# A rotary embedding whose swapped copy is made by ScalarE copies of 32 rows, in place of a TensorE product with a turning matrix

## What is computed

```
def rope(x, pos):
    d = x.shape[-1]
    inv = ROPE_THETA ** (-jnp.arange(0, d, 2, dtype=jnp.float32) / d)
    ang = pos.astype(jnp.float32)[..., None] * inv
    cos = jnp.cos(ang)[:, :, None, :]
    sin = jnp.sin(ang)[:, :, None, :]
    xf = x.astype(jnp.float32)
    x1, x2 = xf[..., : d // 2], xf[..., d // 2:]
    return jnp.concatenate([x1 * cos - x2 * sin, x2 * cos + x1 * sin], axis=-1).astype(x.dtype)
```

## Time and profile before

| what | value |
|---|---|
| runs of the kernel | 2344.1, 2350.22, 2351.34 us (median 2350.22) |
| span of the profiled execution, first to last instruction | 2342.2 us |
| TensorE matmuls | 2255.8 us busy, 96% of the span |
| VectorE | 921.2 us, 39% |
| ScalarE | 381.2 us, 16% |
| mean granted TensorE clock | 0.982 of full speed |

### The profile page before, as it was taken

How to read it: one execution, slowest core, us unless ns; L and a number is a source line. 1 busy time by engine, 2 the same in 40 slices (tenths; PEclk the granted TensorE clock), 3 DMA queues, 4 the chain that set the end, 5 groups by cost and what they waited for, 6 DMA issues and landing times.

```text
span 2342.2 us, 36220 instructions
## 1 busy us (share of the span) xinstructions
PE 2255.8 (96%) x15501; PEld 1588.4 (68%) x15502; DVE 921.2 (39%) x2174; ACT 381.2 (16%) x893; POOL 27.5 (1%) x52
## 2 busy tenths in 40 slices
PE   7999999999999999998999999989999999999999
PEld 5867998877764434433444444357679998769999
DVE  3673887548320000000000000034657744547764
ACT  3231100022220000000000000024421002531100
POOL 1010000001000000000000000000000000000000
PEclk8998999999899999999999999999999999999999
DMA  9562578934069999999988999992325463333541
GB/s 350 188 216 72 174 241 311 377 134 144 6 259 377 373 411 410 409 411 409 407 301 353 409 410 409 412 331 98 109 72 180 153 201 108 134 108 108 171 155 54
DMA packets 242163, 582.98 MB, mean 249 GB/s; under 512 B 24250, under 2 KB 108738, under 8 KB 229716
## 3 DMA queue, kind: packets, MB, share of 16 engines
q1 hardware_dynamic: 241428, 580.52, 66.9%
q0 software_dynamic: 576, 0.13, 0.0%
HBM read 579.58 MB, written 1.05 MB: 248 GB/s over the span
## 4 chain that ended last, share of the span: by engine, by line
PE 84%; DMA 7%; DVE 5%; SPq 2%; ACT 1%; issue 1%; DVEq 0%; ACTq 0%
PE wrk L2507 12%; PE acc L877 8%; PE acc L3314 5%; PE acc L3346 5%; PE acc L2567 5%; DMA ring<-in_moe_w_gate_dram 4%; PE wrk L2492 4%; PE wrk L3346 4%; PE wrk L3314 4%; PE acc L880 3%; PE acc L1658 3%; PE wrk L2514 3%; PE acc L1678 3%; PE wrk L1658 3%; PE acc L954 2%; PE acc L2550 2%
## 5 line engine op out<-in xcount | busy, mean ns | idle before, releaser
L2507 PE MATMUL wrk<-ring,hT 128*64 128x512 f32 (+1 forms) x1792 | 348.7, 542 | 11.7 <-DMA ring<-in_moe_w_up_dram 5.8
L2751 DVE TENSOR_TENSOR scratch<-scratch,wrk 128x512 f32<-128x512 f32 (+4 forms) x32 | 24.5, 767 | 793.0 <-PE wrk L2507 584.5
L2507 PEld LDWEIGHTS wrk<-ring,hT 128*64 128x64 f32 x1792 | 125.8, 137 | 211.6 <-issue 186.2
L877 PE MATMUL acc<-hT,ring 128*128 128x256 f32 x1024 | 231.4, 380 | 0.8 <-DVE hT L852 0.4
L877 PEld LDWEIGHTS acc<-hT,ring 128*128 128x128 f32 x1024 | 191.4, 190 | 29.8 <-issue 3.5
L2567 PE MATMUL acc<-ring,scratch 128*64 128x512 f32 x784 | 177.2, 597 | 8.5 <-DMA ring<-in_moe_w_down_dram 7.8
L3391 DVE TENSOR_TENSOR ring<-ring 128x512 f32<-128x512 f32 (+1 forms) x192 | 155.2, 862 | 1.2
L2567 PEld LDWEIGHTS acc<-ring,scratch 128*64 128x64 f32 x784 | 53.8, 136 | 113.0 <-issue 101.7
L3346 PE MATMUL acc<-scratch,ring 128*128 128x128 f32 x1024 | 117.6, 275 | 0.0
L3346 PEld LDWEIGHTS acc<-scratch,ring 128*128 128x128 f32 x1024 | 116.0, 192 | 0.0
L2686 ACT ACTIVATE scratch<-wrk 128x512 f32<-128x512 f32 (+4 forms) x32 | 21.1, 661 | 483.5 <-PE wrk L2539 483.5
(11 more groups left out here) (464 smaller groups left out, 2983.0 us busy)
## 6 DMA issues: line engine op xcount, KB each, us to landing
ring<-in_moe_w_gate_dram SPq DMA_DIRECT2D x56, 2048.0 KB, 19.0
ring<-in_moe_w_up_dram SPq DMA_DIRECT2D x56, 2048.0 KB, 21.2
ring<-in_moe_w_down_dram SPq DMA_DIRECT2D x56, 2048.0 KB, 22.5
ring<-in_w_ada_dram SPq DMA_DIRECT2D x24, 2048.0 KB, 17.0
ring<-in_w_up_dram SPq DMA_DIRECT2D x32, 1024.0 KB, 6.6
ring<-in_w_down_dram SPq DMA_DIRECT2D x32, 1024.0 KB, 6.7
ring<-in_w_out_dram SPq DMA_DIRECT2D x8, 2048.0 KB, 8.2
ring<-in_w_in_dram SPq DMA_DIRECT2D x10, 1536.0 KB, 9.8
```

Source lines behind the costliest of these rows:

```text
L877: mm = pe.matmul(acc[p0:p0 + m, bank, 0:S], cols(k), hT[:, k, :], start=(k == 0), stop=(k == KD - 1))
L2507: mm = pe.matmul(flat_wrk[h * HD:h * HD + HD, lo:lo + n2], hT[:, k, 0:HD], w[:, at_, h * n2:(h + 1) * n2], start=(k == 0), stop=(k == KD - ...
```

## The change

The tiles that rotate whole halves (7 in a layer of block 1, 6 in a layer of block 2, 26 in all) no longer get a product on TensorE. ScalarE copies the tile in blocks of 32 rows into the temporary that the sine product would have written, each block to its partner's place: four copies for a tile of 128 rows, two for the 64 rows of `rq0` and `rk0`, 96 in all. The minus sign goes into the table: the rate of a head's first half is negative, so its sine is negative and its cosine is unchanged. VectorE then multiplies that copy with the table in place. ScalarE waits, ahead of its copies, for the rotation that used the same temporary last. The PSUM bank of such a step is no longer used, and the steps behind it wait for the bank's reader before it. The 24 rotations of 16 and 32 entries stay as they were.

```
-    add("turn64", turn((0, 64), 0, 32))
...
-            v[h + at:h + at + dim // 2, 0] = inv
+            v[h + at:h + at + dim // 2, 0] = -inv if signed else inv
...
+        def rope_swap_act(act, tag, i, entry, tile_ready, room):
+
+            name, tile, turn, tab, p0, rows = entry
+            place = rope_tmp[2 * (i % 2) + 1]
+            act.wait_ge(*tile_ready)
+            if room:
+                act.wait_ge(*room)
+            for q in range(rows // 32):
+                ins = act.activation(place[p0 + 32 * q:p0 + 32 * q + 32], tile[32 * (q ^ 1):32 * (q ^ 1) + 32], ACT.Copy)
+                ins.then_inc(act_done, up("act", "swapped", tag, name) if q == rows // 32 - 1 else up("act"))
...
-            dve.wait_ge(pe_done, at("pe", "rope", tag, name))
-            dve.tensor_tensor(b, acc[p0:p0 + rows, bank, 0:S], table[p0:p0 + rows, tab, 1, :], ALU.mult)\
-               .then_inc(dve_done, up("dve"))
+            if swapped(entry):
+                dve.wait_ge(act_done, at("act", "swapped", tag, name))
+                dve.tensor_tensor(b, b, table[p0:p0 + rows, tab, 1, :], ALU.mult).then_inc(dve_done, up("dve"))
...
-            users = [i for i in range(n) if step1_bank(l, i) == bank]
+            users = [i for i in range(n) if step1_bank(l, i) == bank and steps1(l)[i][0] != "r"]
...
+            if swapped(rope_step(l, name)[2]):
+                return step_read(l, n - 2)
...
+            elif kind == "r":
+                tag, i, entry, ready = rope_step(l, name)
+                if swapped(entry):
+                    rope_swap_act(act, tag, i, entry, ready, rope_room(l, n, i))
```

More of the change, by code:

```diff
@@ L65, in turn, with rates @@
         return m
-    add("turn64", turn((0, 64), 0, 32))
     add("turn16", turn((0, 64), 0, 8))
     add("turn32", turn((0,), 64, 16))
-    def rates(theta, dim, heads, at, width=P):
+    def rates(theta, dim, heads, at, width=P, signed=False):
         v = np.zeros((P, 1), np.float32)
@@ L74, in rates @@
         for h in heads:
-            v[h + at:h + at + dim // 2, 0] = inv
+            v[h + at:h + at + dim // 2, 0] = -inv if signed else inv
             v[h + at + dim // 2:h + at + dim, 0] = inv
         return v
-    add("rate64", rates(10000.0, 64, (0, 64), 0))
+    add("rate64", rates(10000.0, 64, (0, 64), 0, signed=True))
     add("rate16", rates(500000.0, 16, (0, 64), 0))
@@ L923, in rope_tile_pe, with swapped @@
               .then_inc(pe_done, up("pe", "rope", tag, name))
+        def swapped(entry):
+            return entry[2] == "halves"
+        def rope_swap_act(act, tag, i, entry, tile_ready, room):
[7 more added lines that the diff above has]
+                ins.then_inc(act_done, up("act", "swapped", tag, name) if q == rows // 32 - 1 else up("act"))
         def rope_tile_dve(dve, tag, i, entry, bank, tile_ready):
@@ L931, in rope_tile_dve @@
             dve.tensor_tensor(a, tile, table[p0:p0 + rows, tab, 0, :], ALU.mult).then_inc(dve_done, up("dve"))
-            dve.wait_ge(pe_done, at("pe", "rope", tag, name))
-            dve.tensor_tensor(b, acc[p0:p0 + rows, bank, 0:S], table[p0:p0 + rows, tab, 1, :], ALU.mult)\
-               .then_inc(dve_done, up("dve"))
+            if swapped(entry):
+                dve.wait_ge(act_done, at("act", "swapped", tag, name))
+                dve.tensor_tensor(b, b, table[p0:p0 + rows, tab, 1, :], ALU.mult).then_inc(dve_done, up("dve"))
+            else:
+                dve.wait_ge(pe_done, at("pe", "rope", tag, name))
+                dve.tensor_tensor(b, acc[p0:p0 + rows, bank, 0:S], table[p0:p0 + rows, tab, 1, :], ALU.mult)\
+                   .then_inc(dve_done, up("dve"))
             settle(dve, "dve", dve_done)
             dve.tensor_tensor(tile, a, b, ALU.add).then_inc(dve_done, up("dve", "rope", tag, name))
[L938 to L945, removed]
         def outproj_first_pe(pe, item, h, ms, ks):
@@ L1191, in rope1 @@
             tiles += [(f"aq{j}", s_q[:, j, :]) for j in range(3)]
-            return [(name, tile, "turn64", 0, 0, P) for name, tile in tiles]
+            return [(name, tile, "halves", 0, 0, P) for name, tile in tiles]
         def index_pe(pe, l, pair):
@@ L1857, in step1_read @@
                 return act_done, at("act", "ada parts", int(name))
-            if kind == "s":
-                return dve_done, at("dve", "mods", 0, int(name))
-            return dve_done, at("dve", "rope", ("1", l), name)
+            return dve_done, at("dve", "mods", 0, int(name))
         def rope1_entry(l, name):
@@ L1886, in step1_pe @@
                 ada_sum_pe(pe, int(name), acc[:, bank, 0:4], bank_read)
-            else:
-                i, entry, ready = rope1_entry(l, name)
-                rope_tile_pe(pe, ("1", l), entry, bank, bank_read, ready)
         def step1_act(act, l, step):
@@ L1904, in step1_act @@
                 ada_vec_act(act, int(name), step1_bank(l, n))
+            elif kind == "r":
+                i, entry, ready = rope1_entry(l, name)
+                rope_swap_act(act, ("1", l), i, entry, ready, (dve_done, at("dve", "rope", ("1", l), rope1(l)[i - 2][0])) if i >= 2 else None)
         def step1_dve(dve, l, step):
@@ L2844, in rope2 @@
             for n, z in (("rq", t_q), ("rk", t_k)):
-                plan += [(n + "0", z[HD:P, 0, :], "turn64", 1, HD, HD)]
-                plan += [(f"{n}{j}", z[:, j, :], "turn64", 1, 0, P) for j in (1, 2)]
+                plan += [(n + "0", z[HD:P, 0, :], "halves", 1, HD, HD)]
+                plan += [(f"{n}{j}", z[:, j, :], "halves", 1, 0, P) for j in (1, 2)]
             return plan
@@ L3000, in rope_step, with rope_room @@
             return ("2", l), i, plan[i], (act_done, at("act", "proj", ("2", l), name))
+        def rope_room(l, n, i):
+            before = [rope_step(l, step.partition(" ")[2]) for step in STEPS[:n] if step[0] == "r"]
+            tag, _, entry, _ = [step for step in before if step[1] % 2 == i % 2][-1]
+            return dve_done, at("dve", "rope", tag, entry[0])
         def step_read(l, n):
@@ L3026, in step_pe @@
                 tag, i, entry, ready = rope_step(l, name)
-                rope_tile_pe(pe, tag, entry, bank, bank_read, ready)
+                if not swapped(entry):
+                    rope_tile_pe(pe, tag, entry, bank, bank_read, ready)
             elif kind == "sums":
```

## The result

The changed kernel is slower: 2369.43 us median of four runs (2365.80 to 2374.09) against 2347.77 of the kernel before (four runs by then; the forecast stood on three with a median of 2350.22), ratio 1.0099, 95% interval 1.0085 to 1.0113. The forecast was 2352 us, range 2345 to 2360. The profiled execution (2374.09 us) was the longest of its four, that of before the shortest of its four, so their spans differ by 29.9 us where the medians differ by 21.7. Lines have moved: copies L936, sine product of a copied tile L948, sum L954, evacuations L909, index products L1213 and L1215, band products L1388, turned probabilities L1161 (ScalarE), values L1064.

What follows compares the result with a forecast made beforehand. TensorE was taken to bound the kernel (matmuls 2255.8 of 2342.2 us), with VectorE setting the band stretch. Block 1's +3.3 and block 2's -1.3 gave +2.0, 2344.2; with the median 8.0 above that span, 2352 us, range 2345 to 2360.

Steps and rivals of the forecast that it cites:

- What one copy costs: Price of a 32x256 ScalarE copy: 0.31 us start to start, four in 1.33 us, twelve in 3.81 us.
- the walk through ScalarE's list: Going through the timeline at each rotation: +1.65 us a layer in block 1, -0.65 in block 2.
- aq0 to aq2: Block 1's band stretch: removing these products gains nothing, and their copies, done while VectorE is busy, cost nothing.
- the tail of block 2: Block 2's last rotations, rk1, rk2 and rk0, at the end of attention: -0.45 us a layer.
- the pieces are dearer: Rival: copies dearer because they change partitions and each raises a count; step 0.45 makes the sum 7.0 us; chance 0.13.
- Index rotations: Block 1, iq0, iq1, ik: TensorE waits for the last of twelve copies, starting index products 0.35 us later a layer.
- ak: Block 1, band 4: copies behind the "p aq0" copy let VectorE go on later, +1.3 us a layer.
- Block 2: All rotations of block 2's attention: -0.65 us a layer, -1.3 us for two layers.
- rq1 and rq2: Two rotations in block 2: TensorE gains 0.5 us at the first and loses 0.3 at the second, a layer.
- The clock: Rival: TensorE falls to 1.2 GHz in one or two more stretches, 1.6 us each, 2354 to 2355 us; chance 0.16.
- Full return: Rival: all TensorE time of the 26 removed products comes back, 11.7 us less, 2338.5 us; chance 0.11.
- signs of error: Wrong if bands' end stays when ak moves, twelve copies take 5 us or more, or block 1 shows new lower-clock stretches.

Runs made afterwards that it cites:

- the probe: Changed kernel with block 1's seven copies cut in other patterns, rotated rows wrong, to read copy prices only; iq0 stepped 0.43 us; no kernel time given.
- three-piece kernel: Changed kernel with three copies a tile instead of four, upper half of 128-row tiles left unswapped, 1.29 us a tile: 2363.10 us, ratio 1.0061.
- the change once more: The changed kernel run again unaltered, on the chip of the runs with extra products: 2369.21 us, ratio 1.0095 to the kernel before.
- the fillers: Changed kernel plus unread extra TensorE products while it waits ahead of the index products: 5 gave 2365.03 us, 18 gave 2371.45 us.
- the tail moved: Changed kernel, all copies kept, block 1's copies and block 2's three rk tiles' copies earlier in ScalarE's list: 2344.73 us, ratio 0.9989.

## Why the prediction was wrong

The step that failed first is "What one copy costs", and the larger failure is the walk through ScalarE's list behind it, which put aq0 to aq2 at nothing, the tail of block 2 at a gain and the clock outside the sum. The 0.31 us came from copies that all sit on the same 32 rows, and I carried it over to pieces that each start on other rows; the term measured 0.44. The budget of 0.51 us a piece from the Trainium skill, page "ScalarE: Activation LUTs", section "Rules for kernel authors", is given there for an instruction whose bias is a pointer operand; these copies measured 0.41 us long and 0.44 from start to start. The rival "the pieces are dearer" was the true one in its price, and not in its reason: iq0 of the probe changes no partitions and is as dear (0.43). But its own sum, 2 + 36 x 0.13 = 6.7 us, 2357 us, still misses by 12: the three-piece kernel, near the forecast's price, had 2363.1 us where 2352 was forecast. So the terms of place were mis-sized too:

- **Index rotations, +0.35 a layer.** Right in kind; with three pieces +0.5, with four +1.8 (21.6 - 19.8). Not in the sum: the half clock behind the wait, 1.6 us more (band 0: 44.2 - 40.8 = 3.4 in all).
- **ak, +1.3 a layer.** Right at its price: with three pieces the wait grows by 2.61 - 1.31 = 1.3, and from band 0 to band 6 layer 1 takes (71.1 - 41.3) - (69.3 - 40.8) = 1.3 longer. With the true price it is (74.5 - 44.2) - (69.3 - 40.8) = 1.8.
- **aq0 to aq2, "they cost nothing either".** A term put at nothing that measured 3.0 us a layer. It holds for aq0 and aq1 in layer 1 (in layer 0 aq1 waited 0.96 us), but aq2's copies stand behind the table load and the copy of "p bg0", and VectorE had no other work to do there (its wait of 1.32 us): bands 8 to 11 grew by (99.8 - 85.1) - (91.5 - 79.8) = 3.0 us, part of it the half clock.
- **Block 2, -1.3.** rq1 and rq2 together as forecast, near nothing: with block 2 alone changed, layer 1's last scores start 0.3 us earlier than before (126.9 for 127.2 us from the block's start). The tail, "-0.45", was wrong in sign: I followed rk0's rotation to VectorE, and not what queued behind its copies on ScalarE, the last copy of turned probabilities. In executions where no half clock follows, it costs nearly nothing (the change once more had 143.4 us to out 2 in layer 1); in others 2 to 6 us.
- **The clock, 1.6 us a stretch, chance 0.16.** The mechanism was named, its frequency was not: I made it "one or two more" stretches, independent of the sum. At the index products the fillers show that it follows from the wait that the sum itself adds; for the other stretches that is not shown.
- **Full return.** Dead: with one copy of 0.41 us a tile the time is that of before. With the tail moved band 11 of layer 1 comes 2.7 us earlier than before (88.8 for 91.5) and out 1 only 0.4 (152.9 for 153.3), so what the products give back is used up in waits between.

The prediction's own signs of error, twelve copies in 5 us or more and lower-clock stretches in block 1, both came.

## What to carry to other kernels

A step that moves to an idle engine costs what its place in that engine's list makes it cost: here the same 96 copies cost 21 to 22 us in one order of ScalarE's list and nothing in another, so read, at each place, what the moved instructions stand behind, and what stands behind them. Take the price of an instruction from a row with the same sequence of rows and places, not only the same shape. Where a change adds a wait of TensorE (2.4 us here), price the projection behind it at the lower clock too.

## What the hardware showed that I had not expected

In these runs two ScalarE copies in a row overlap only when they read and write at the same block of 32 rows: 64-column copies of 0.24 us then start every 0.15 us, and every 0.27 when only the read moves. The Trainium skill, page "ScalarE: Activation LUTs", section "What ACT_TABLE_LOAD costs", says that back-to-back ACTIVATEs overlap by about 93 ns. The trace agrees for copies on one block (0.24 - 0.15 = 0.09) and not for the others. For VectorE the Trainium skill, page "VectorE: DVE Perf Modes", section "Two Vector instructions with no wait between them", states such a rule by start quadrants of 32 partitions; these runs show its like on ScalarE.
